# Decays of the next chunk's first two groups moved ahead of the last gate copy in a chunked SSD scan

## What is computed

```python
def step(state, inp):
    xc, ac, bc, cc = inp
    cs = jnp.cumsum(ac, axis=1)
    seg = cs[:, :, None] - cs[:, None, :]
    lmat = jnp.exp(jnp.where(causal, seg, -jnp.inf))
    cb = jnp.einsum("blgn,bsgn->blsg", cc, bc)
    y_diag = jnp.einsum("blsg,blsgj,bsgjp->blgjp", cb, lmat, xc)
    y_off = jnp.einsum("blgn,bgjpn,blgj->blgjp", cc, state, jnp.exp(cs))
    decay = jnp.exp(cs[:, -1:] - cs)
    new_state = (state * jnp.exp(cs[:, -1])[..., None, None]
                 + jnp.einsum("blgn,blgj,blgjp->bgjpn", bc, decay, xc))
    return new_state, y_diag + y_off
```

## Time and profile before

| | us |
|---|---|
| three runs, median (lowest to highest) | 3249.74 (3247.03 to 3251.0) |
| profiled execution, its own time | 3249.21 |
| its span, first to last instruction | 3247.6 |
| TensorE busy (share of the span) | 3074.1 (95%) |
| VectorE busy | 1071.6 (33%) |
| ScalarE busy | 861.0 (27%) |
| GpSimd busy | 752.0 (23%) |

### The profile page before, as it was taken

The page is one execution under the profiler, slowest core; times in us unless marked ns, Lnnn a source line. Parts: engine busy times, 40 slices in busy tenths (PEclk is TensorE's granted clock), DMA queues, the critical chain, the costliest instruction groups (busy, mean ns, idle before and its releaser), DMA issues. The chain is left out here.

```text
span 3247.6 us, 41561 instructions
## 1 busy us (share of the span) xinstructions
PE 3074.1 (95%) x15182; PEld 2586.7 (80%) x15182; DVE 1071.6 (33%) x1824; ACT 861.0 (27%) x1461; POOL 752.0 (23%) x390
## 2 busy tenths in 40 slices
PE   6999999999999999999998999998999968989898
PEld 5888888888888888888887778777898856778687
DVE  6003444201000011110001544444565567762333
ACT  5110000000000000000112555554566542332232
POOL 7111111111111111112322443442111034321000
PEclk9999999999999999999999999998999989999999
DMA  5121121344412201112234564564534457775543
GB/s 156 58 77 65 71 77 68 93 117 129 116 59 77 77 20 38 39 39 86 97 97 132 148 174 136 155 174 171 157 119 144 144 176 237 235 244 145 174 136 116
DMA packets 335884, 387.70 MB, mean 119 GB/s; under 512 B 23104, under 2 KB 284480, under 8 KB 320192
## 3 DMA queue, kind: packets, MB, share of 16 engines
q1 hardware_dynamic: 317440, 287.42, 30.0%
q10 hardware_dynamic: 16080, 91.23, 8.1%
q0 software_dynamic: 2304, 8.39, 0.7%
HBM read 251.21 MB, written 135.79 MB: 119 GB/s over the span
## 5 line engine op out<-in xcount | busy, mean ns | idle before, releaser
L286 PE MATMUL p_acc<-h,w_hi 128*128 128x512 f32 x2464 | 970.0, 394 | 3.8 <-DVE h L496 3.5
L288 PE MATMUL p_acc<-h,w_lo 128*128 128x512 f32 x2464 | 966.0, 392 | 0.0
L287 PE MATMUL p_acc<-h,w_hi 128*128 128x512 f32 x2464 | 960.2, 390 | 0.0
L288 PEld LDWEIGHTS p_acc<-h,w_lo 128*128 128x128 f32 x2464 | 463.1, 188 | 103.9
L286 PEld LDWEIGHTS p_acc<-h,w_hi 128*128 128x128 f32 x2464 | 463.7, 188 | 100.5 <-DVE h L496 4.8
L287 PEld LDWEIGHTS p_acc<-h,w_hi 128*128 128x128 f32 x2464 | 463.3, 188 | 101.0
L247 POOL CAST w_hi<-raw 128x1024 fp32r<-128x1024 f32 x88 | 91.4, 1039 | 1350.9 <-PE p_acc L288 1344.9
L1598 PE MATMUL b_acc<-b_yhi,b_whi 128*128 128x512 f32 x512 | 205.7, 402 | 43.8 <-DVE b_ylo_ssd L1689 25.8
L249 POOL TENSOR_TENSOR w_lo<-raw,w_hi 128x1024 fp32r<-128x1024 f32 x88 | 212.1, 2410 | 7.1
L393 ACT ACTIVATE p_stage<-p_acc 128x1024 f32<-128x1024 f32 (+1 forms) x45 | 64.2, 1427 | 554.3 <-PE p_acc L288 554.2
L1600 PE MATMUL b_acc<-b_yhi,b_wlo 128*128 128x512 f32 x512 | 202.6, 396 | 0.0
(11 more groups left out here) (195 smaller groups left out, 4141.4 us busy)
## 6 DMA issues: line engine op xcount, KB each, us to landing
raw<-w_in SPq DMA_DIRECT2D x113, 512.0 KB, 4.4
a_q<-s_qs SPq DMA_DIRECT2D x27, 1024.0 KB, 4.9
b_gate<-s_gates SPq DMA_DIRECT2D x48, 512.0 KB, 7.1
s_xbc<-p_stage ACTq DMA_DIRECT2D x16, 1024.0 KB, 3.9
work<-s_xbc SPq DMA_DIRECT2D x16, 1024.0 KB, 7.1
s_sums<-s_cs SPq DMA_DIRECT2D x16, 1024.0 KB, 5.1
b_att<-s_att SPq DMA_DIRECT2D x24, 528.0 KB, 5.6
s_qs<-p_stage ACTq DMA_DIRECT2D x24, 512.0 KB, 5.5
```

What stands on the lines that cost most here:

```text
L286: pe.matmul(to, w_hi[:, slot, c], h_hi, start=c == 0, stop=False)
L287: pe.matmul(to, w_hi[:, slot, c], h_lo, start=False, stop=False)
L288: last = pe.matmul(to, w_lo[:, slot, c], h_hi, start=False, stop=c == KC - 1)
```

## The change

Only ScalarE's program changes. `decays` takes the chunk as an argument. The decays of groups 0 and 1 are no longer made behind the B copy of their own chunk; they are made at the end of the chunk before, behind the Sqrt and ahead of the third gate copy and the output copy. The first chunk's are made ahead of the loop. The last chunk makes none ahead, so the last pair is written out behind a loop over seven pairs. Decays 2 now stand between the B copy and the first gate copy. Waits and semaphore counts of each decay stay as they were, with the chunk's own number.

```diff
-                with act.Fori(0, PAIRS) as i:
+                def decays(c, g):
+                    if g == 0:
+                        act.wait_ge(sums_loaded, 16 * c + 16)
+                    act.wait_ge(mix_made, 4 * c + g + 1)
+                    for j in range(4):
+                        last = act.activation(fall[:, g % 2, j], sums[:, 4 * g + j], ACT.Relu,
+                                              bias=cs[:, bass.ds(c * HEADS + 4 * g + j, 1)], scale=-1.0)
+                    last.then_inc(fall_made, 1)
+                    act.wait_ge(fall_made, 4 * c + g + 1)
+                    act.activation(fall[:, g % 2], fall[:, g % 2], ACT.Exp, scale=-1.0).then_inc(decay_made, 1)
+
+                def chunks(i, last_pair):
                     for k in range(2):
...
                         act.activation(b_tok[:], ps_m[:, :BANK], ACT.Copy).then_inc(b_tok_ready, 1)
-                        decays(0)
-                        decays(1)
+                        decays(c, 2)
                         take_item(3 * k)
-                        decays(2)
-                        decays(3)
+                        decays(c, 3)
                         take_item(3 * k + 1)
...
                         act.activation(std[:], ss[:], ACT.Sqrt, bias=eps[:], scale=1.0 / GW).then_inc(std_made, 1)
+                        if not (last_pair and k):
+                            decays(c + 1, 0)
+                            decays(c + 1, 1)
                         take_item(3 * k + 2)
...
+                decays(0, 0)
+                decays(0, 1)
+                with act.Fori(0, PAIRS - 1) as i:
+                    chunks(i, False)
+                chunks(PAIRS - 1, True)
```

More of the change, by code:

```diff
@@ L857, in take_item @@
                             act.activation(g_out[:, j % 2], acc[:], ACT.Copy).then_inc(item_taken, 1)
[L859 to L868, removed]
                         act.wait_ge(x_transposed, c + 1)
```

## The result

| | before | changed |
|---|---|---|
| profiled execution, its own time | 3249.21 | 3323.68 |
| its span | 3247.6 | 3322.1 |
| last chunk, L802 starts behind the output copy at | 2211.97 | 2266.10 |
| attention stage, first matmul | 2254.16 | 2309.92 |
| TensorE busy | 3074.1 | 3107.4 |

The changed kernel takes 3318.7 us (median of four runs, 3313.5 to 3324.8), 69.0 more than the kernel before. Its ratio to the kernel before is 1.0214, 95% interval 1.0185 to 1.0244: slower by 2.1%. The forecast was 3305.6, in a range of 3280 to 3324. Four executions that took far longer than the rest of their kernel (one of the kernel before at 4392 us, three of the run with early sums at 3490 us and more) are left out of every median here.

What follows compares the result with a forecast made beforehand. TensorE's own order was taken to bound each chunk, with the mix and the output copy as doors. 59.1 + 25.5 - 31.4 + 2.7 = +55.9 on 3249.21, medians 0.53 higher, gave 3305.6 us, range 3280 to 3324.

Steps and rivals of the forecast that it cites:

- The bound and the delay: Chunk ends: late sums and the decay block make the output copy 3.94 us late, 15 times, +59.1 us.
- The clock: Behind TensorE's 4.2 us idle at L802: one slow stretch of 1.7 us a boundary, +25.5 us.
- the rival with the longer slow stretch: Behind the idle at L802: 0.6 us more at each of 15 boundaries, 3315 us, chance 0.13.
- What is given back: Groups 0 and 3: mix waits of the 15 later chunks and five slow stretches go, -31.4 us.
- The rival in which they only move behind GpSimd: Mixes queue behind GpSimd's instructions, about 1 us of waits a chunk stays, 3321 us, chance 0.10.
- Chunk 0: Decays made before the first x copy, with table loads, start group 0 later: +2.7 us.
- The scan's sum: Scan stage: delay, clock, waits given back and first chunk add up to +55.9 us.
- the base: Whole kernel: the profiled 3249.21 us to which the scan's sum is added, with only the scan stage touched.
- The rivals with the table load: ScalarE's decay block: load inside the wait for sums, 3286 us, chance 0.07; load drains first, 3325 us, chance 0.04.

Runs made afterwards that it cites:

- the run with early sums: Changed kernel, but SyncE loads the next chunk's sums ahead of its wait for the second gate copy: 3246.9 us, ratio 1.0003.
- the one with the short block and late sums: Changed kernel with only group 0's decays made ahead, group 1's behind the B copy, sums loaded as in the kernel before: 3265.7 us, ratio 1.0054.
- The filled idle: Changed kernel with 16 matmuls, results unread, in TensorE's order between the transposes of x and the wait for the output copy: 3281.3 us, ratio 1.0097.
- the run with one group ahead: Changed kernel with sums loaded earlier, only group 0's decays ahead, group 1's behind the B copy, group 2's behind the first gate copy: 3249.8 us, ratio 1.0007.
- one or two idle copies: Changed kernel with one or two Copy of 128 x 1024 at the end of ScalarE's scan program: ratio 1.0158 with one, 1.0156 with two.
- the kernel with one line moved: Kernel before with group 2's decays moved ahead of the first gate copy, nothing made ahead, sums late: 3232.0 us, ratio 0.9946.

## Why the prediction was right, and where it was not

**The bound and the delay: right.** TensorE's order set the chunk. Forecast was an output copy 3.94 us late and a wait of 4.2 us at L802, 15 times; measured were 4.06 and 4.2 (63.1 us in all, 59.1 + 3.6 forecast). The Relu waited 2.4 to 2.5 us for the sums, and the block took 4.96. The run with early sums and the one with the short block and late sums (2.4 us expected, 2.44 measured) show that the two causes add up as in the sum.

**The clock: right in kind, undersized.** One slow stretch a boundary, put at 1.7 us. From L802 to group 0 the changed kernel takes 7.26 us, 5.16 without waits at full clock: 2.1. The filled idle shows it is the clock. That is nearer to the 2.3 of the rival with the longer slow stretch than to the 1.7 of the sum.

**What is given back: right.** The waits for the mix fell by 23.9 us: 22.9 in the later chunks, which have none left, as forecast, and 1.0 in chunk 0. The rival in which they only move behind GpSimd fell for this order, but the run with one group ahead shows it to be real: there group 3's waits grew from 7.3 to 18.5 us.

**Chunk 0: wrong.** Forecast +2.7. Group 0 starts at 1759.05, where it was 1759.22. The step that failed is the table loads. The loop-top load that I expected to stay is gone in every chunk. The likely reason is that with the decays at the end of the loop's body Exp's table is in on both ways into it:

```profile
L886 ACT ACT_TABLE_LOAD x16 | 20.5, 1283 | 0.3
L859 ACT ACT_TABLE_LOAD x15 | 19.2, 1283 | 0.3
```

That is one load fewer than before (8 at L872, 8 at L868, 16 at L888), and none at the first decays. Two loads less are 2.6 us, and the first Relu started another 0.9 us earlier than in the kernel before, at 1751.51, because the sums had landed by then.

**The scan's sum** was +55.9; the start of attention moved by +55.8. So close a hit is luck, for it is closer than its terms: measured they are 59.5 (waits at L802) + 31.5 (15 x 2.1) - 23.9 - 8.5 (five former slow stretches) = +58.6. Chunk 0's mix wait is inside the 23.9, and 2.8 us are placed nowhere.

**What lay behind the scan: missing.** The sum took the later stages as fixed. In the profiled execution they cost 18.7 us more, and of the total's 69.0 us some 13 to 15 are of this kind: with one or two idle copies the same scan ends at 3303 to 3304 us, 1.6% above the kernel before. This step, the base, failed: the time of the kernel before holds a stage whose length changes by up to 24 us from one kernel or execution to the next. The measured 3318.7 is in the range of 3280 to 3324, but beyond the forecast's own 3295 to 3313, and the room above was there for a longer slow stretch or waits that move, not for this. (The lower of these two bounds doesn't follow from the landing either: with 4.9 us instead of 5.1 the sum gives 3302.6.) The profile could have shown a part of it: the clock was at 0.93 in the 100 us of attention above although TensorE was busy for 91.7 of them.

**The rivals with the table load** are out, both the one that it drains first and the one that it runs inside the wait for the sums: in the timeline above the load follows the Relu by 0.02 us and the Exp follows the load by 0.01.

## To carry to other kernels

Before work is moved into an engine's gap, put the start of its latest input into the gap first, a load issued by a queue that waits for something else above all; here moving the load by one line was worth 68 us. A small idle of TensorE costs more than its length when the clock falls behind it: here 15 waits of 4.2 us cost 2.1 us more each, while 15 of 1.7 us left the clock alone. And a gain or loss in one stage is to be read at the start of the next: the total can give it back, or add to it, in a stage that nobody touched. An experiment that is meant to delay something must be checked in its own trace first: the idle copies here fell into a wait and delayed nothing.

## What was not expected of the hardware

- The attention stage, instruction for instruction the same, takes 360 to 384 us (span of the scores matmuls) in different kernels and executions. One part goes with the granted clock, 0.97 to 0.80 over the 100 us from 26 us behind its start, with TensorE just as busy; another is a wait for ScalarE's probabilities, 0.8 to 11.4 us.
- The same changed scan was measured at 3318.7 us and, with idle copies that delay nothing, at 3303 and 3304 in another session. What made the 15 us isn't shown.
- Idles of 2 us ahead of group 0 brought the clock down in five of six chunks of the kernel before and in one of five in the kernel with one line moved. How long TensorE idles doesn't decide it alone.
